# Two fused transformer blocks: low parts of the output weights on VectorE, high parts one unit sooner, and ten of 48 modulation products moved into a later stage

## What is computed

```
h = h + 0.5 * swiglu(rmsnorm(h), w1, w3, w2)            # ffn1, 22 tiles of 128 hidden columns
z = rmsnorm(h) @ w_in                                   # attention (compressed, selected, window) and an S5 mixer
h = h + concatenate([o_nsa, o_s5]) @ w_out              # "wout": 8 column tiles
h = h + 0.5 * swiglu(rmsnorm(h), w1, w3, w2)            # ffn2, again 22 tiles
h = h + sigmoid(rmsnorm(h) @ w_ple_gate) * (p @ w_ple);  x = rmsnorm(h)
for l in range(2):                                      # second block
    shift, scale, gate     = split(silu(c)    @ w_mod[l] + b_mod[l])    # modulation, for x
    shift_c, scale_c, gate_c = split(silu(c_ctx) @ w_mod[l] + b_mod[l]) # and for the context
    ... retention, differential attention, chunk MLP on modulate(x) and modulate(ctx) ...
    y = sum_b sigmoid(mlog_b) * (o_b @ w_bo[b]);  out = y @ w_o          # the merge
    x = x + gate * rms_norm(out, g_post)
```

## Time and profile before

| | |
|---|---|
| median of 3 runs | 1555.39 us (1555.1 to 1556.11) |
| the profiled execution | 1554.36 us, its span 1552.6 us |
| PE busy | 1493.6 us (96%), 10100 matmuls |
| weight load (PEld) busy | 1324.8 us (85%) |
| DVE, ACT, POOL busy | 939.8 us (61%), 726.7 us (47%), 104.6 us (7%) |
| granted TensorE clock, mean of the span | 0.995 |

### The profile page before, as it was taken

One profiled execution on the slowest core, in us unless ns is written; L12 is line 12 of the kernel. 1 busy time (PEld: TensorE's weight loads), 2 busy tenths in 40 slices (PEclk: granted clock), 3 DMA queues, 4 the chain that ended last, 5 costly groups with the idle time before them and its releaser, 6 DMA issues.

```text
span 1552.6 us, 26109 instructions
## 1 busy us (share of the span) xinstructions
PE 1493.6 (96%) x10100; PEld 1324.8 (85%) x10100; DVE 939.8 (61%) x1487; ACT 726.7 (47%) x1256; POOL 104.6 (7%) x137
## 2 busy tenths in 40 slices
PE   6999999989999999999999999999999999999997
PEld 6999989669999997787777778888878887889997
DVE  5788778654777786875654436334235635556664
ACT  5444465356444456336545364222245436556444
POOL 3800000013000000001000000000000002010000
PEclk9999999999999999999999999999999999999999
DMA  8766645415777754442221222333332332225663
GB/s 294 225 203 200 205 153 172 155 58 201 237 237 240 244 171 155 148 164 68 68 69 55 68 69 95 108 109 108 97 102 87 109 109 71 91 91 177 208 206 123
DMA packets 74728, 223.25 MB, mean 144 GB/s; under 512 B 6672, under 2 KB 26128, under 8 KB 74128
## 3 DMA queue, kind: packets, MB, share of 16 engines
q1 hardware_dynamic: 54672, 195.20, 38.7%
q10 hardware_dynamic: 19968, 26.82, 5.2%
HBM read 220.94 MB, written 1.05 MB: 143 GB/s over the span
## 4 chain that ended last, share of the span: by engine, by line
PE 80%; DVE 8%; DMA 5%; ACT 5%; issue 2%; SPq 0%; POOL 0%; DVEq 0%; ACTq 0%
PE ps L496 67%; DMA ring<-stream 5%; PE ps L509 3%; DVE w_lo L428 2%; ACT w_hi L1257 2%; PE ps L997 1%; PE ps L1013 1%; PE ps L1005 1%; PE ps L1081 1%; PE ps L1070 1%; PE ps L970 1%; DVE mod_junk L1860 0%; PE ps L1050 0%; DVE area L1840 0%; DMA pk<-pack 0%
## 5 line engine op out<-in xcount | busy, mean ns | idle before, releaser
L496 PE MATMUL ps<-hn_hi,w_hi 128*128 128x256 f32 (+1 forms) x1895 | 607.2, 320 | 18.0 <-DVE w_lo L428 7.8
L496 PE MATMUL ps<-hn_hi,w_lo 128*128 128x256 f32 (+1 forms) x1895 | 592.1, 312 | 0.0
L496 PE MATMUL ps<-hn_lo,w_hi 128*128 128x256 f32 (+1 forms) x1895 | 591.9, 312 | 0.0
L428 DVE TENSOR_TENSOR w_lo<-ring,w_hi 128x1024 fp32r<-128x1024 f32 (+1 forms) x339 | 405.5, 1202 | 302.6 <-ACT w_hi L1257 299.1
L1257 ACT ACTIVATE w_hi<-ring 128x1024 fp32r<-128x1024 f32 (+1 forms) x347 | 359.8, 1038 | 325.2 <-DMA ring<-stream 241.2
L496 PEld LDWEIGHTS ps<-hn_hi,w_hi 128*128 128x128 f32 x1895 | 361.0, 191 | 48.1 <-DVE w_lo L428 12.8
L496 PEld LDWEIGHTS ps<-hn_hi,w_lo 128*128 128x128 f32 x1895 | 361.1, 191 | 21.3
L496 PEld LDWEIGHTS ps<-hn_lo,w_hi 128*128 128x128 f32 x1895 | 361.2, 191 | 21.2 <-issue 1.0
L1325 ACT ACTIVATE area<-ps 128x512 f32<-128x512 f32 (+1 forms) x136 | 67.2, 507 | 212.1 <-PE ps L496 211.9
L496 PE MATMUL ps<-area_r,w_hi 128*128 128x256 f32 (+1 forms) x578 | 135.4, 328 | 0.8 <-ACT area L1325 0.6
L496 PEld LDWEIGHTS ps<-area_r,w_hi 128*128 128x128 f32 x578 | 96.1, 188 | 14.0 <-issue 2.9
(11 more groups left out here) (324 smaller groups left out, 1616.4 us busy)
## 6 DMA issues: line engine op xcount, KB each, us to landing
ring<-stream SPq DMA_DIRECT2D x359, 512.0 KB, 3.8
mod_at<-mod_stream ACTq DMA_DIRECT2D x34, 512.0 KB, 5.4
area<-mod_stream ACTq DMA_DIRECT2D x12, 512.0 KB, 5.4
pk<-pack ACTq DMA_DIRECT2D x1, 1610.0 KB, 7.2
pk<-pack SPq DMA_DIRECT2D x1, 1549.0 KB, 12.3
h<-x_in SPq DMA_DIRECT2D x1, 1024.0 KB, 4.8
cond_at<-cond SPq DMA_DIRECT2D x2, 512.0 KB, 14.2
mod_at<-mod_stream SPq DMA_DIRECT2D x2, 512.0 KB, 12.5
```

The costliest lines, as they stand in the source:

```text
L428: eng.tensor_tensor(lo[:, 0:w], raw, hi[:, 0:w].bitcast(F32), ALU.subtract).then_inc(lo_ready[who], 1)
L496: m = pe.matmul(dst, w_, x_, start=(start and n == 0), stop=(stop and n == 2), skip_group_check=True)
```

## The change

1. The low parts of wout go from POOL to DVE. Units 0 and 1 are split between the probabilities of the last head pairs, unit 2 before the first residual add, and unit j + 2 after the add of tile j.
2. In the wout loop ACT prepares the high parts one unit sooner.
3. `scores(1)` stands ahead of `compress(3)`.
4. ffn2 makes 12 modulation products instead of 22 (one for two tiles). The 12 at the head of layer 0 stay where they are, as numbers 26 to 37. The last ten are made in the merge of layer 0, three in each of the steps 1, 2 and 3 and one in step 4, with loads of their own that ACT issues, and `finish_mods(1)` follows there.
5. The kept conditions get other places: the one for x goes into a new tile `masks`, which the two mask matrices `negc` and `idb` used before; the one for the context is moved by ACT into the place of `pT`, once the second block's values need its first place. POOL makes its two copies at other times: after the S5 output, and after the last scores.

```diff
-LATE_MOD = FFN_MODS[1] + FT
+LATE_MOD = FFN_MODS[1] + 2 * ((FT - 2) // 4) + 2
+MERGE_MOD = LATE_MOD + 12
...
-LOW = {}
-for _name in SPLIT_UNITS:
-    _who = "pool" if _name[0] == "wout" else "dve"
-    LOW[_name] = (_who, 1 + sum(1 for w, _ in LOW.values() if w == _who))
+LOW = {name: ("dve", n + 1) for n, name in enumerate(SPLIT_UNITS)}
...
+        def load_merge_mod(eng, m):
+
+            if m >= MERGE_MOD + 2:
+                eng.wait_ge(s("mod_used"), m - 1)
+            eng.dma_start(merge_slot(m), mod_stream[m]).then_inc(s(f"merge_loaded{m % 2}"), 16)
...
             compress(2)
+            scores(1)
             compress(3)
-            scores(1)
...
-                            load_mod(act, m0 + f + 1, 4 * it)
+                            if f % 2 == 1:
+                                load_mod(act, m0 + 2 + f // 2, 2 * it)
...
             for k in range(KT):
-                prepare(("wout", k))
+                prepare(("wout", min(k + 1, KT - 1)))
                 squares(2, h, dve_evac, [n_wout + k for k in range(KT)], range(k, k + 1))
...
                     if l == 0 and slot == 4:
-                        act.wait_ge(s("mod_used"), MODS)
+                        act.activation(merge_cond(1), late_cond(1), ACT.Copy).then_inc(s("cond_moved"), 1)
+                        act.wait_ge(s("mod_used"), MERGE_MOD)
...
+                        if l == 0 and f > 0 and MERGE_MOD + 3 * f + b - 1 < MODS:
+                            load_merge_mod(act, MERGE_MOD + 3 * f + b - 1)
...
-                            modulation(m0 + f, 4 * it)
+                            if f % 2 == 0:
+                                modulation(m0 + f // 2, 2 * it)
...
+                if p == 4:
+                    low_until(("wout", 0))
                 if p >= 3 and p % 2 == 1:
                     o_low((p - 3) // 2)
+                if p == 5:
+                    low_until(("wout", 1))
+            low_until(("wout", 2))
             for j in range(KT):
                 product(dve, "wout", j)
                 tt_(h[:, j, :], h[:, j, :], bank(BANK["wout", j][0], 0, T), ALU.add).then_inc(dve_evac, 1)
+                if 1 <= j < KT - 2:
+                    low_until(("wout", j + 2))
...
                 for f in range(KT):
+                    if l == 0 and 1 <= f < 4:
+                        modulation(MERGE_MOD + 3 * f - 3)
+                        modulation(MERGE_MOD + 3 * f - 2)
+                        low_until(("mlog", l, 2, f))
+                        modulation(MERGE_MOD + 3 * f - 1)
+                    if l == 0 and f == 4:
+                        modulation(MODS - 1)
+                        finish_mods(1)
                     low_until(("wbo", l, f, 1))
...
-            low_until(("wout", KT - 1))
...
-            for st in range(2):
-                pool.tensor_copy(late_cond(st), cond_silu(st)).then_inc(s("cond_kept"), 1)
+            pool.tensor_copy(late_cond(1), cond_silu(1)).then_inc(s("cond_kept"), 1)
+            pool.wait_ge(s("scored"), 8)
+            pool.tensor_copy(late_cond(0), cond_silu(0)).then_inc(s("cond_kept"), 1)
```

More of the change, by code:

```diff
@@ L105 @@
 FU = 3 * FT
-LOW = {}
-for _name in SPLIT_UNITS:
-    _who = "pool" if _name[0] == "wout" else "dve"
-    LOW[_name] = (_who, 1 + sum(1 for w, _ in LOW.values() if w == _who))
+LOW = {name: ("dve", n + 1) for n, name in enumerate(SPLIT_UNITS)}
 PACK = [
     ("g_ffn1", 8), ("g_mix", 8), ("g_ffn2", 8), ("g_ple", 8), ("g_final", 8), ("g_pre", 16), ("g_post", 16),
-    ("b_mod", 48), ("pT", 512), ("ident", 128), ("ones", 128), ("rot64", 128), ("steps", 256),
+    ("b_mod", 48), ("ident", 128), ("ones", 128), ("rot64", 128), ("steps", 256), ("pT", 512),
 ]
@@ L246, in two_block_kernel @@
         eps = sb("eps", [P, 1])
-        negc = sb("negc", [P, P], BF16)
-        idb = sb("idb", [P, P], BF16)
+        masks = sb("masks", [P, 4 * T])
+        negc = masks[:, 0:P // 2].bitcast(BF16)
+        idb = masks[:, P // 2:P].bitcast(BF16)
         mods = sb("mods", [P, LAYERS, 3 * KT, 2])
@@ L738, in scores @@
                 for g in range(2):
-                    pe.matmul(o[g][:, 0:P], idb[:, :], negc[:, :], start=False, stop=True, skip_group_check=True)
-                    m = pe.matmul(o[g][:, 2 * P:3 * P], idb[:, :], negc[:, :], start=False, stop=True, skip_group_check=True)
+                    pe.matmul(o[g][:, 0:P], idb, negc, start=False, stop=True, skip_group_check=True)
+                    m = pe.matmul(o[g][:, 2 * P:3 * P], idb, negc, start=False, stop=True, skip_group_check=True)
                 m.then_inc(s("scored"), 1)
@@ L1259, in high_part @@
                 late = u - UNIT["dk", 0, 3] + LATE_MOD
-                if LATE_MOD + 3 <= late < MODS:
+                if LATE_MOD + 3 <= late < MERGE_MOD:
                     load_late_mod(act, late)
@@ L1764, in _ @@
                 branch_high(l, 1)
+                if l == 0:
+                    act.wait_ge(s("ret_scaled"), RET_AT[1])
+                    for m in range(MERGE_MOD, MERGE_MOD + 2):
+                        load_merge_mod(act, m)
                 def y_high(k):
@@ L1770, in _ @@
                 for f in range(KT):
+                    if l == 0 and f == 4:
+                        act.wait_ge(s("mod_used"), MODS - 1)
                     if 2 <= f < (5 if l == 0 else KT):
@@ L1850, in modulation @@
                     dve.wait_ge(s(f"mod_loaded{m % 2}"), 16 * (m // 2 + 1) + 8 * body)
+                elif 0 in halves and m < MERGE_MOD:
+                    dve.wait_ge(s(f"late_loaded{m % 3}"), 16 * ((m - LATE_MOD) // 3 + 1))
                 elif 0 in halves:
-                    dve.wait_ge(s(f"late_loaded{m % 3}"), 16 * ((m - LATE_MOD) // 3 + 1))
+                    dve.wait_ge(s(f"merge_loaded{m % 2}"), 16 * ((m - MERGE_MOD) // 2 + 1))
+                if m == MERGE_MOD:
+                    dve.wait_ge(s("cond_moved"), 1)
                 if m == 0:
@@ L1858, in modulation @@
                 w, silu = (mod_slot(m), cond_silu) if m < LATE_MOD else (late_mod_slot(m), late_cond)
+                if m >= MERGE_MOD:
+                    w, silu = merge_slot(m), merge_cond
                 if 0 in halves:
@@ L2001, in ffn @@
                 else:
-                    modulation(m0 + FT - 1)
+                    modulation(LATE_MOD - 1)
                 product(dve, tag, "w2", FT - 1)
@@ L2013, in _ @@
             ffn("ffn1", 0)
-            dve.tensor_copy(negc[:, :], c("causal")).then_inc(masks_ready, 1)
-            dve.tensor_copy(idb[:, :], c("ident")).then_inc(masks_ready, 1)
+            dve.tensor_copy(negc, c("causal")).then_inc(masks_ready, 1)
+            dve.tensor_copy(idb, c("ident")).then_inc(masks_ready, 1)
             low_until(("u", 1))
@@ L2427, in _ @@
                             low_until(name)
-                            if late[0] < MODS:
+                            if late[0] < MERGE_MOD:
                                 modulation(late[0])
@@ L2433, in _ @@
                 if l == 0:
-                    while late[0] < MODS:
+                    while late[0] < MERGE_MOD:
                         modulation(late[0])
                         late[0] += 1
-                    finish_mods(1)
                 for slot, name in enumerate(slot_units(l)):
@@ L2539, in link @@
                 pool.wait_ge(pool_step, steps[0])
-            made = [0]
-            def low_until(name, past=0):
-                for v in SPLIT_UNITS:
-                    who, count = LOW[v]
-                    if who == "pool" and count > made[0] and UNIT[v] <= UNIT[name] + past:
-                        low_part(pool, v)
-                        made[0] = count
             tt_, ts = pool.tensor_tensor, pool.tensor_scalar
```

7 lines of the change are left out of this document (5 added, 2 removed).

## The result

The changed kernel takes 1547.09 us (median of 6 runs, 1543.25 to 1550.95), the kernel before beside it 1555.75 us (6 runs, 1553.62 to 1556.88). The ratio is 0.9944 with a 95% interval of 0.9927 to 0.996: 8.7 us faster, between 6 and 11 us. A later series of the changed kernel gave 1544.87 us and 0.9927 (0.9911 to 0.9943). The forecast was 1547.6 us; the profiled execution took 1544.42 us, where the sum had asked for 1546.6.

What follows compares the result with a forecast made beforehand. PE was taken as the bound, busy 96% of the span, with gains where it waits. Terms 1.1 + 2.6 - 0.3 + 1.2 + 1.5 + 1.7 = 7.8 us off 1554.36, plus 1.03, gave 1547.6 us; range 1543.5 to 1552.

Steps and rivals of the forecast that it cites:

- Scores ahead of the compression: First block: scores(1) fits into PE's 1.47 us wait at compress(3); 1.1 us less, ends 1.0 and 1.2.
- POOL away from beside DVE: First block: DVE instructions slowed beside POOL's low parts return to normal times; 2.6 us less, ends 0 and 3.3.
- POOL's copies: POOL's two copies at new times contend with DVE's two-input instructions; 0.3 us lost, between 0 and 1.0 us.
- The clock: Half-speed stretch from 316.6 to 323.4 us costs 2.4 us and may go; 1.2 us less, ends 0 and 2.4.
- wout: Six wout units lose 2.0 us; unit 3's wait goes, unit 4 waits about 0.5 us; 1.5 us less, ends 0.5 and 2.0.
- ffn2: Ten products and loads leave ffn2, cutting PE's 3.6 us of low-part waits; 1.7 us less, between 0 and 3.3.
- The merge: Layer 0's merge takes the moved products with 0.6 us of slack, three times, so 0 us.
- rival 4: Merge stalls if modulation loads land later than 5.4 us; were the three 10 us, 4.2 us slower, 1559.6 us; chance 0.04.
- the first (clock up, all of ffn2): Clock doesn't fall and loads are all there was in ffn2; 10.6 us less, 1544.8 us; chance 0.18.
- the main case: Whole kernel, each term near its middle: 7.8 us less, 1547.6 us, spanning 1544.5 to 1550.5 us; chance 0.57.

Runs made afterwards that it cites:

- pool_late: Kernel before, with POOL keeping its low parts of wout but starting them only when all eight passes' probabilities are made: 1551.65 us, ratio 0.9967.
- dve_low: Kernel before, with wout's low parts on DVE and high parts one unit sooner, without the scores(1) exchange or the ten moved products: 1548.03 us, ratio 0.9959.
- fill_wait: Kernel before, with the matmuls of scores(4) issued twice to fill PE's wait ahead of weigh(0): 1552.29 us, ratio 0.9979.
- not_sooner: Changed kernel with the high parts of wout prepared at their old steps: 1545.88 us, ratio 0.9943.
- loads_kept: Changed kernel with eleven loads put back into ffn2, into an area that nobody reads: 1550.39 us, ratio 0.9962.

## Why the prediction was right, and where it was not

The total is right by the median, 1547.09 us against 1547.6. The profiled execution was 2.2 us better than the sum, and it lies below its own median by 2.67 us, where that of the kernel before lies 1.03 us below. The six runs of the changed kernel spread over 7.7 us. Where and how often the clock falls is one part of that (one of its two traces has a half-speed stretch near 815 us, the other none before 1536 us), but a stretch cost 1.5 or 2.3 us where it was measured, so the rest of the spread is open. That the two differences all but cancelled is luck: the profiled execution gained 9.9 us where the sum has 7.8. By its terms:

- **Scores ahead of the compression: 1.1 us predicted, 0 to 0.4 measured.** The step that failed is "so it fits into the wait". It fits, but what counts is when compress(3)'s load lands, and the wait had a second customer: the gate product stands 0.47 us behind compress(3) as soon as nothing is between them. From compress(3)'s start to the gate product's it was 2.95 us (294.14 to 297.09, in the first row below) and is 2.40, so 0.55 us at most, less what compress(3) starts later. Alone it gave nothing; beside the other edits the S5 output to weigh(0) takes 26.7 to 27.0 us instead of 27.23 to 27.33, so about 0.4.
- **POOL away from beside DVE: 2.6 us predicted, 2.7 to 2.8 measured** (30.00 to 27.33 in pool_late, 27.23 in dve_low). Right, and so was keeping something back: of DVE's own 3.3 us some 0.6 don't come through. The rule that the Trainium skill states in "SBUF — State Buffer", section "Who interferes with whom", that a DVE instruction with two SBUF inputs contends with a GpSimd instruction that reads SBUF, is borne out by pool_late, where nothing else was moved.
- **POOL's copies: -0.3 us predicted, nothing seen.** The one at 324.10 lay beside two instructions that take PSUM as an input, which took 0.42 and 0.41 us as ever.
- **The clock: 1.2 us predicted, 2.3 in the changed kernel's profiles.** The cost of the fall (2.4 us) was right, by fill_wait 2.3; the middle value stood for not knowing whether it stays. Over nine profiles with the wait of 2.07 us it stayed away in six and cost 1.5 us in three, so the mean gain is 2.3 - 1.5 / 3 = 1.8 us. The wait did not go, as predicted (about 2 us); that it no longer brought the clock down each time was left to chance in the forecast, and why 2.07 us does it one time in three and 2.27 did it each time, with the waits ahead of it also larger, is open.
- **wout: 1.5 us predicted, 1.26 measured.** Unit 3's wait went and unit 4 is 0.4 us late, as worked out. The 2.0 us said to be lost were 1.66, because the row at 345.41 holds two adds and so 0.36 us that no wait causes: 1.66 - 0.40 = 1.26. That the high parts must come sooner for it was not right: not_sooner has 18.12 us.
- **ffn2: 1.7 us predicted, 3.5 in the pair of profiles, 3.9 in the mean.** The end of the range (3.3) was nearer than its middle. That the loads matter more than DVE's work fits the runs and isn't settled: loads_kept gave all of it back, DVE's work back cost 0.2 to 2.8 us. The step that failed took PEld's 3.6 us of waits as all that isn't hidden: from the first to the last down step the layer took 175.60 - 169.6 = 6.0 us more than its tiles need.
- **The merge: 0 us, right.** The slack was 2.7 us, not 0.6: the third product starts 7.3 us behind DVE's end of the step before (975.62 + 0.69 = 976.31 to 983.59 in the rows below), where 996.2 - 986.7 = 9.5 had been worked out. Two terms were too large. The landing was taken at 5.4 us; it took 4.2 in these steps (the late loads' median is 4.8 in the page after). And 1.0 us was put between the start of ACT's take and the load's issue, where both rows have 979.42. (The end at 986.7 is that of step 1, not of step 0; the steps are alike, 24.74 us apart, so nothing hangs on it.) So rival 4 would have needed more than 2 us more than it was given.

The first row is of the kernel before, the others of the changed one:

```profile
297.09 1.95 PE L783 MATMUL ps<-area,ring 128*128 128x256 f32 x8
...
975.62 0.69 DVE L2561 TENSOR_TENSOR area<-area 128x512 f32<-128x512 f32 x1
...
979.42 0.60 ACT L1334 ACTIVATE area<-ps 128x512 f32<-128x512 f32 x1 [3.29 <-PE ps L504]
979.42 0.34 ACTq L448 DMA_DIRECT2D area<-mod_stream  x1
...
983.59 1.23 DVE L1884 SCALAR_TENSOR_TENSOR mod_junk<-area,masks 128x1024 bf16<-128x1024 f32 x1 [1.12 <-DMA area<-mod_stream]
```

Of the rivals, the first (clock up, all of ffn2) is what the profiled executions of the changed kernel show, with 1544.42 us and, in the second series, 1543.27 us; the median of the first series lies nearer to the main case.

## What to carry to other kernels

When an instruction takes several times what the same shape takes elsewhere in the trace, look at the other engine's timeline at that moment before its operands: moving POOL's two-input work out of those 5 us gave 5.1 of the change's 9 to 11 us, with what the clock gave back. A wait that can't be removed can be made cheaper by work of no use, where it brings PE's clock down; and a wait filled with work from behind it is worth only what remains once the next step in the queue shows its own wait. A probe that adds a buffer is cleaner if it adds it last, so that nothing else moves.

## What the runs showed of the hardware that was not expected

- A buffer of 8 bytes a partition ahead of others made the matmuls that read the gated rows 281 ns instead of 277, so that a tile with no wait took 8.58 us instead of 8.48, with nothing else changed. What it costs the whole kernel is not shown: 1550.65 against 1546.46 us by the medians, 1550.35 against 1550.17 us in the profiled executions.
- Extra matmuls without use made the kernel before 3.3 us faster (1.4 to 5.1).
- Apart from the last 6 to 9 us of each span, the half-speed stretches lasted some 3.4 or 6.8 us, and all but two in the fourteen traces began near one of four places: 17 us (5 traces), 317 (6), 613 (2) and 815 to 825 (7). Which of them an execution shows varies: near 815 us in one profile of the changed kernel, nowhere before 1536 us in the other.
